# RWKV-7 and stick-breaking layer, projection phase: bonus sums from high and low parts, one buffer for the mixing's differences

## The reference, cut to what matters

```python
h = concat(meta_tokens, x)                      # 16 + 2048 tokens, D_MODEL 1024
proj = rms_norm(h, pre_norm_g) @ w_in           # r,k,v + low-rank parts, gate, q,k,v,gate, merge
u = u + (u_prev - u) * mu                       # token shift ("mixing") of r, k, v, w_lo, a_lo
decay = exp(-DECAY_SCALE * sigmoid(w0 + tanh(w_lo) @ w_up))
a = sigmoid(a0 + a_lo @ a_up)
kk = k * k_k ; kk = kk * rsqrt(sum_head(kk * kk) + eps)
k = k * (1 + (a - 1) * k_a)
...                                             # recurrence over tokens, group norm -> y
bonus = sum_head(r * k * r_k) * v               # <- the sum that the change touches
y = (y + bonus) * silu(g_rwkv)
...                                             # stick-breaking attention, merge, output projection
```

## Time and profile before

| | us |
|---|---|
| median of 3 runs | 4174.6 (4170.5 to 4175.4) |
| profiled execution, its own time | 4176.6 |
| its span | 4174.8 |
| TensorE busy in the span | 4015.3 (96%) |
| VectorE, ScalarE, GpSimd busy | 2326.7, 1708.9, 816.8 |
| half A of the projection | about 0 to 1023 |
| half B of the projection | about 1023 to 2010 |

### The profile page before, as it was taken

The page is one execution under the profiler, slowest core; times in us unless marked ns, Lnnn a source line. Parts: engine busy times, 40 slices in busy tenths (PEclk is TensorE's granted clock), DMA queues, the critical chain, the costliest instruction groups (busy, mean ns, idle before and its releaser), DMA issues. The chain is left out here.

```text
span 4174.8 us, 88869 instructions
## 1 busy us (share of the span) xinstructions
PE 4015.3 (96%) x34728; PEld 3319.8 (80%) x34728; DVE 2326.7 (56%) x3166; ACT 1708.9 (41%) x3428; POOL 816.8 (20%) x658
## 2 busy tenths in 40 slices
PE   7999999998899999999799999999899999999999
PEld 6888998887688888888566666666789888878887
DVE  6344545434543444444578888888567777633222
ACT  4222322222322222222376767677556565521111
POOL 3101111110211001111000000000256666600222
PEclk9999999999899999999899999999999999999999
DMA  2433333334233443433543444443333333365653
GB/s 92 119 119 116 116 103 99 106 114 153 63 109 113 121 121 115 120 106 115 131 94 86 84 94 100 98 98 78 89 112 109 104 108 108 86 219 166 208 176 126
DMA packets 482562, 479.67 MB, mean 115 GB/s; under 512 B 256784, under 2 KB 366992, under 8 KB 476128
## 3 DMA queue, kind: packets, MB, share of 16 engines
q1 hardware_dynamic: 469360, 445.85, 38.4%
q10 hardware_dynamic: 11520, 25.17, 1.7%
q0 software_dynamic: 1392, 4.54, 0.5%
HBM read 305.51 MB, written 169.93 MB: 114 GB/s over the span
## 5 line engine op out<-in xcount | busy, mean ns | idle before, releaser
L1251 ACT ACTIVATE keep<-z 128x512 f32<-128x512 f32 (+4 forms) x704 | 366.9, 532 | 182.6 <-PE z L1195 177.7
L1289 DVE TENSOR_TENSOR_SCAN kept<-keep,kept 128x512 f32<-128x512 f32 (+2 forms) x448 | 404.0, 952 | 22.5 <-ACT keep L1251 15.8
L1261 ACT COPY w<-turned 128x512 f32<-128x512 f32 (+4 forms) x704 | 367.2, 548 | 103.1 <-PE turned L1205 102.5
L1205 PE MATMUL turned<-t_identity,kept 128*128 128x128 f32 (+1 forms) x2432 | 372.8, 276 | 31.8 <-DVE kept L1289 17.1
L1205 PEld LDWEIGHTS turned<-t_identity,kept 128*128 128x128 f32 (+1 forms) x2432 | 280.5, 135 | 106.5 <-ACT w L1261 24.3
L1286 DVE TENSOR_TENSOR_SCAN kept<-keep,hidden 128x512 f32<-128x512 f32 (+3 forms) x256 | 275.0, 1114 | 153.2 <-ACT keep L1251 152.4
L1194 PE MATMUL z<-k_high,q_parts 128*128 128x512 f32 (+4 forms) x704 | 298.5, 425 | 19.6 <-DMA k_low<-scr_k_lo 12.7
L1232 PE MATMUL acc<-w,dv 128*64 128x512 f32 (+3 forms) x1280 | 289.6, 540 | 0.0
L1195 PE MATMUL z<-k_low,q_parts 128*128 128x512 f32 (+4 forms) x704 | 252.8, 360 | 0.0
L1772 POOL TENSOR_TENSOR off<-NT,tri 128x512 f32<-128x512 f32 x165 | 205.6, 1272 | 141.4 <-ACT NT L1666 141.4
L1232 PEld LDWEIGHTS acc<-w,dv 128*64 128x64 f32 x1280 | 94.7, 137 | 135.4 <-issue 116.4
(11 more groups left out here) (572 smaller groups left out, 10875.1 us busy)
## 6 DMA issues: line engine op xcount, KB each, us to landing
w_raw0A<-in_w_main SPq DMA_DIRECT2D x42, 512.0 KB, 3.8
w_raw0B<-in_w_main SPq DMA_DIRECT2D x42, 512.0 KB, 3.9
w_raw1A<-in_w_main SPq DMA_DIRECT2D x41, 512.0 KB, 3.9
w_raw1B<-in_w_main SPq DMA_DIRECT2D x41, 512.0 KB, 3.9
KB<-scr_kb SPq DMA_DIRECT2D x33, 512.0 KB, 5.2
AR<-scr_ar SPq DMA_DIRECT2D x33, 512.0 KB, 5.9
y_raw<-scr_y SPq DMA_DIRECT2D x64, 256.0 KB, 4.5
merge<-scr_merge SPq DMA_DIRECT2D x64, 256.0 KB, 5.5
```

Of the source, the lines that this page charges most:

```text
L1205: mm = pe.transpose(turned[num % TB][0:size, P * r:P * r + P], kept[kept_in(g)][:, src:src + size], t["identity"][:, :])
L1251: act.activation(keep[num % KB][:, 0:size], z[num % ZB][:, 0:size], ACT.Sigmoid, scale=-DH ** -0.5).then_inc(keep_done, 1)
L1261: act.copy(w[num % WB][0:size, c0:512], turned[num % TB][0:size, c0:512]).then_inc(copied, 1)
L1289: dve.tensor_tensor_scan(dst, data, data, kept[kept_in(g)][:, end:end + 1], ALU.mult, ALU.bypass).then_inc(scanned, 1)
```

## The change

The bonus terms are split like the squares of `norm`: ScalarE copies them into a rounded tile `bonus_hi`, VectorE writes the difference `bonus_lo`, and TensorE sums both with two fp32r products that accumulate in the same bank, instead of one plain fp32 product. The two new tiles hold one group each, so ScalarE's copy of a group waits for the product of the group before (`bonus_pe`). ScalarE's copy stands at the head of each group of `BKS`, ahead of its wait for that group's product. VectorE's difference stands at the head of each group of `BKS`, behind the split of the next weights. The three difference buffers of the mixing become one, and a shift waits for the shift just before it. Some semaphores are joined: `pool_go` and `sp_go` into `go`, `constants` into `preset`, `inverted` into `normed` (which then counts two for each tile).

```diff
-        difs = [sb(f"dif{b}", [P, max(size for _, size in SG)]) for b in range(3)]
+        dif = sb("dif", [P, max(size for _, size in SG)])
+        bonus_parts = [sb(f"bonus_{x}", [P, max(size for _, size in SG)], F32R) for x in ("hi", "lo")]
...
             def bonus_sum(k, g, at, size):
-                now(pe, rk_done, k, g)
+                now(pe, bonus_high, k, g)
+                now(pe, bonus_low, k, g)
                 if g:
                     now(pe, bonus_done, k, g - 1)
                 else:
                     now(pe, sig_done, k, G - 1)
-                pe.matmul(low_bank[:, 0:size], t["ones_sum"][:, :].bitcast(F32), bonus[:, at:at + size], start=True, stop=True).then_inc(bonus_pe, 1)
+                pe.matmul(low_bank[:, 0:size], t["ones_sum"][:, :], bonus_parts[0][:, 0:size], start=True, stop=False)
+                pe.matmul(low_bank[:, 0:size], t["ones_sum"][:, :], bonus_parts[1][:, 0:size], start=False,
+                          stop=True).then_inc(bonus_pe, 1)
...
+            def high_bonuses(k, g, at, size):
+                now(act, rk_done, k, g)
+                if g:
+                    now(act, bonus_pe, k, g - 1)
+                else:
+                    past(act, bonus_pe, k, G - 1)
+                act.copy(bonus_parts[0][:, 0:size], bonus[:, at:at + size]).then_inc(bonus_high, 1)
...
                     i = AT[BKS] + g
+                    high_bonuses(k, g, at, size)
                     made(act, k, i)
...
-                dif, z = difs[x % 3], lead(at)
-                dve.wait_ge(mixed, count + 3 * G - 3)
+                z = lead(at)
+                dve.wait_ge(mixed, count + 3 * G - 1)
...
+            def low_bonuses(k, g, at, size):
+                now(dve, bonus_high, k, g)
+                dve.tensor_tensor(bonus_parts[1][:, 0:size], bonus[:, at:at + size], bonus_parts[0][:, 0:size].bitcast(F32),
+                                  ALU.subtract).then_inc(bonus_low, 1)
...
                         if j == BKS:
+                            low_bonuses(k, g, at, size)
                             operands(k, g, at, size)
                             bonuses(k, g, at, size)
                             key_lows(k, g, at, size)
```

More of the change, by code:

```diff
@@ L120, in project_phase @@
         r_done, a_done, b_done, rk_done = s_("rop"), s_("aop"), s_("bop"), s_("rk")
+        bonus_high, bonus_low = s_("bonus_high"), s_("bonus_low")
         bonus_pe, bonus_done, bg_done, gg_done = s_("bonus_pe"), s_("bonus"), s_("bg"), s_("gg")
         vt_pe, vt_out, vst_pe, vst_out = s_("vt_pe"), s_("vt_out"), s_("vst_pe"), s_("vst_out")
-        pool_go, sp_go = s_("pool_go"), s_("sp_go")
+        go = s_("go")
+        PRESET = 6 if opening else 2
         ar_sent, kb_sent, vt_sent, vst_sent = s_("ar_sent"), s_("kb_sent"), s_("vt_sent"), s_("vst_sent")
@@ L129, in project_phase @@
         x_in = [s_(f"x_in{b}") for b in range(4)]
-        summed, rooted, inverted, normed = s_("summed"), s_("rooted"), s_("inverted"), s_("normed")
+        summed, rooted, normed = s_("summed"), s_("rooted"), s_("normed")
         turned, gained_done, tile_high, tile_low = s_("turned"), s_("gained"), s_("tile_high"), s_("tile_low")
@@ L133, in project_phase @@
             const_in, par_in, rest_in = s_("const_in"), s_("par_in"), s_("rest_in")
[L134 removed]
+            adjusted, ones_done = s_("adjusted"), s_("ones_done")
         square_high, square_low = q_lo
@@ L194, in store_staged @@
                     evacuated(sp, k, i)
-                    sp.sem_inc(sp_go, 1)
+                    sp.sem_inc(go, 1)
                     c = T0 + at - CHUNK
@@ L214, in load_x @@
                 if n >= 4:
-                    sp.wait_ge(normed, n - 3)
+                    sp.wait_ge(normed, 2 * n - 6)
                 if row is None:
@@ L411, in turn @@
                 row, m, at = tiles[n]
-                pe.wait_ge(normed, n + 1)
+                pe.wait_ge(normed, 2 * n + 2)
                 for part in range(2):
@@ L557, in edges_out @@
                 act.copy(edge[:, :], low_bank[0:PAIRS, 0:P]).then_inc(edge_out, 1)
-            for s in (sig_done, exp_done, sq_done, sq_high, root_done, vt_out, vst_out):
+            for s in (sig_done, exp_done, sq_done, sq_high, root_done, vt_out, vst_out, bonus_high):
                 act.sem_inc(s, G)
@@ L578, in _ @@
             if opening:
-                act.wait_ge(constants, 4)
+                act.wait_ge(preset, 4)
             square_sums(0)
@@ L585, in _ @@
                     tile_high_part(n - 2)
-            act.wait_ge(preset, 2)
+            act.wait_ge(preset, PRESET)
             if opening:
@@ L735, in normalise @@
                 dve.wait_ge(rooted, n + 1)
-                dve.reciprocal(rinv[0:m, n:n + 1], std[0:m, n:n + 1]).then_inc(inverted, 1)
-                dve.wait_ge(inverted, n + 1)
+                dve.reciprocal(rinv[0:m, n:n + 1], std[0:m, n:n + 1]).then_inc(normed, 1)
+                dve.wait_ge(normed, 2 * n + 1)
                 dve.tensor_scalar(hn[n % 3][0:m, :], x[n % 4][0:m, :], rinv[0:m, n:n + 1], None, ALU.mult).then_inc(normed, 1)
@@ L752, in _ @@
             if opening:
[L753 to L756, removed]
+                dve.memset(t["eps"][:, 0:1], RMS_EPS).then_inc(preset, 1)
+                dve.memset(t["eps"][:, 1:2], GN_EPS).then_inc(preset, 1)
+                dve.memset(t["eps"][:, 2:3], L2_EPS).then_inc(preset, 1)
+                dve.memset(t["carry"][:, :], 0.0).then_inc(preset, 1)
             if opening:
@@ L763, in _ @@
             dve.memset(keep[:, :, 0:1], 1.0).then_inc(preset, 1)
-            dve.wait_ge(preset, 2)
+            dve.wait_ge(preset, PRESET)
             dve.sem_inc(mixed, 3 * G)
-            for s in (sq_low, run_done, rnorm_done, kk_done, r_done, a_done, b_done, rk_done, bonus_done):
+            for s in (bonus_low, sq_low, run_done, rnorm_done, kk_done, r_done, a_done, b_done, rk_done, bonus_done):
                 dve.sem_inc(s, G)
@@ L822, in final_keys @@
                 pool.wait_ge(cols_done, k + 1)
-                pool.sem_inc(pool_go, 1)
+                pool.sem_inc(go, 1)
                 pool.tensor_scalar(gain[:, at:at + size], rate[:, at:at + size], col(K_A),
```

## The result

The changed kernel takes 4239.5 us (median of 4 runs, 4239.1 to 4241.2) against 4173.1 us: ratio 1.0157, 95% interval 1.0142 to 1.0173. It is slower by 66 us; the forecast was 70 us over the median then shown, at 4245, and the time lies in the range. The profiled execution has a span of 4237.3 us, 62.5 more than before.

A forecast was written before the change was run, and what follows sets the result against it. TensorE's queue was taken to bound both loops. Profiled 4176.6 us plus 59.1 stall less 12.8 slots (+46.3) plus 24 clock gave 4246.9, against the median 4245 us (+1.7%); range 4217 to 4263 us.

The forecast's parts named there:

- The stall: Group 0's bonus product waits for VectorE's low part: 4.68 us per pair in A, 2.71 in B, 59.1 us in all.
- Groups 1 and 2: Later bonus products in the key block: no stall, VectorE's low part ready with 2 us spare or more.
- TensorE's loop has no other wait that could shrink: In the two loops, nothing repays the 59.1 us of stall.
- The releaser in the profile: The idle ahead of the first replacing product would be released by VectorE's difference, eight times in each half.
- The slots: Two fp32r products replace one plain fp32: gain 0.83 us per pair in A, 0.78 in B, 12.8 us in all.
- The clock: TensorE at half clock behind stalls, 2.0 us each: all eight in A, 16 us; half of B's, 8 us; +24 us.
- The rule of the Trainium skill: Long idle gaps between matmul bursts lower TensorE's clock; its limit lies between the stalls, so A falls and B does not.
- The sum: Whole kernel: 4176.6 + 46.3 + 24 = 4246.9 us, against the shown median 4245 us, +1.7%.
- the rival in which only A's stalls drop the clock: Both loops stall but half clock follows only in A: 4175 + 46 + 16 = 4237 us; chance 20%.
- The dif buffer and the joined semaphores: One difference buffer instead of three and joined semaphores: edits at nothing; bound for the buffer's shifts 0 to 0.1 us.

The follow-up runs named there:

- the filled kernel: Changed kernel plus matmuls of no use ahead of group 0's wait, 24 in A and 10 in B per stall: ratio 1.0112.
- the one with both parts early: Changed kernel with group 0's ScalarE high part and VectorE low part moved into the query block, ahead of the weight split: ratio 0.9998.
- the wait alone: Kernel before, plain fp32 product kept, but group 0's product waits for VectorE's first operand of that group: 4257.9 us, ratio 1.0193.
- the high part early: Changed kernel with only ScalarE's high part of group 0 moved into the query block: ratio 1.0157.
- the last kernel: Changed kernel, group 0's parts early; in A, group 0's bonus sums times v and group 1's low part ahead of the weight split: 4161.8 us, ratio 0.9960.
- the kernels with the parts early: Changed kernel with group 0's parts early, 0.9998; also A's group 1 low part ahead of group 0's operands, 0.9992; the latter with plain product, 1.0020.

## Why the prediction came out as it did

**The stall: right.** 4.68 and 2.71 us per pair were forecast in terms of slots. The records show gaps of 4.50 and 2.53; the last matmul's record reaches 0.17 us into the next slot, which gives 4.67 and 2.70, 59.0 us in all. Groups 1 and 2 do not stall in the changed kernel, also as forecast. The estimate for them was rough: VectorE did wait for ScalarE's high part of group 1 (1.21 us, until 116.52), and the reserve was that of a kernel that had just stalled. The forecast said nothing of what comes late once the stall is gone. Its sentence that "TensorE's loop has no other wait that could shrink" was wrong by 0.3 us per pair of A: group 1's wait for the bank went, since behind the stall VectorE reads that bank 5.5 us before TensorE asks for it again.

**The releaser in the profile: wrong by the letter.** I wrote that VectorE's difference would be named. The profile says "issue". Of the waits ahead of that product the changed kernel's trace holds only the one for ScalarE's high part, which had ended seven microseconds before. In the filled kernel and in the one with both parts early the same two waits stand in the code, the trace holds the one for VectorE, and VectorE is named. So it is a matter of the record and not of the kernel; why that wait is not in it stays open.

**The slots: right in B, short in A.** B gains 0.80 us per pair (forecast 0.78). A gains 1.15 (forecast 0.83), as the pair of 120.15 us shows. The mis-sized term is that of group 1: I took group 0's slot of 0.64 us for both, and missed the 0.3 us per pair that this product cost beyond it, with the wait for the bank in front. Together 15.6 instead of 12.8 us.

**The clock: right in kind, too dear by 6 us.** Forecast 16 in A and 8 in B, measured 12.8 and 4.9. All of A's fell, as forecast. The price per fall was 1.6 us and not 2.0: this time none had the long form of 3.0 us that the earlier trace rows show once. With the wait alone, half of A's falls had it, so the mean of 2.0 was inside what happens. In B three of eight fell where I took four. The rule of the Trainium skill (TensorE: Matmul & The Clock Gate, "Why this matters for your kernels"), by which A's stalls fall and B's do not, is right for A; in B nine stalls of 24 in three kernels fell at 2.5 to 2.6 us.

**The sum.** A: 37.4 + 12.8 - 9.2 = 41.0; B: 21.6 + 4.9 - 6.4 = 20.1; together 61. The forecast had 70 here, so it is 9 too high, two thirds of that by the clock; that the times lie only 4 us apart (66 against 70) is in part luck, since scatter outside the loops is as large. The measured 4239.5 us is nearer to the 4237 us of the rival in which only A's stalls drop the clock than to the forecast, though three of B's fell as well.

The span grew by 62.5: the opening of A was 3.2 us longer up to the first product (stall taken off; among other things the clock fell there behind a gap of 3.16 us, and in the trace before not behind one of 3.17), and the part behind B's loop some 1.8 us shorter. The buffer and the joined semaphores do touch the opening. But with the same opening the first product came, stall taken off, at 105.7 us in the filled kernel and at 109.5 with the high part early, and with the opening of the kernel before between 105.6 and 108.0 (wait alone). So I take both for scatter, which is argued and not shown. The dif buffer and the joined semaphores show no cost, as forecast: the sum needs none, and the last kernel, which has both, gained the full 16 us. Only the buffer was tried alone.

## What to carry to other kernels

A busy share of 100% says what an engine is bound by, not how much reserve its suppliers have: VectorE was half idle over the loop and without a microsecond to spare at the one place where TensorE asks. Before making an operation cheaper by splitting its operands, look in the supplier's timeline for the end of the last step that will stand ahead of the new one, and put the new step ahead of long work that nobody needs yet (here the next block's weights). When a stall is taken away, look for the next chain behind it, and pay attention to a buffer's release as much as to its operands.

## What was not expected of the hardware

An idle time of one length does not always have one price. At 2.5 to 2.6 us TensorE's clock fell in 9 of 24 stalls, at 2.1 us in 1 of 8, at 4.5 us in 24 of 24, and a fall cost between 1.5 and 3.1 us. Behind the gaps of 1.1 to 1.8 us of the kernels with the parts early it fell in none of 24.

VectorE's difference of 512 columns took 1.40 us where GpSimd's product had begun 0.44 us before it, and 0.68 us elsewhere in the same kernel: from GpSimd's end at 1149.33 to its own at 1149.88 are 0.55 us. The Trainium skill (SBUF — State Buffer, "SBUF: two separate sides") says that a VectorE instruction with two SBUF inputs and a GpSimd instruction hold their common ports for a whole instruction and that the other waits. The row agrees: the difference looks held until GpSimd's product is over. Half A shows the same: beside a product of GpSimd the split's difference took 1.76 us in the changed kernel, and 1.23 us in the last one, where `bonus_lo` lay beside it and took 0.99 instead of 0.55 us. So a step that is moved can also change which step pays.
